# Layer norms by token block, folded scale and shift, an unrolled layer loop, and the next layer's modulation under the feed-forward

## The reference

```python
for l in range(DEPTH):                                  # DEPTH = 2
    mod = c_act @ w_ada[l] + b_ada[l]                   # 6 * 1024 numbers
    sh1, sc1, gt1, sh2, sc2, gt2 = [m[:, None, :] for m in jnp.split(mod, 6, axis=-1)]
    h = x * (1.0 + sc1) + sh1
    y = _token_mixer(h, ...)                            # three attention branches, gates, w_out
    x = _layernorm(ALPHA * x + gt1 * y, ln_g[l, 0], ln_b[l, 0])
    h = x * (1.0 + sc2) + sh2
    y = _conv_ffn(h, w_up[l], w_conv[l], b_conv[l], w_down[l])
    x = _layernorm(ALPHA * x + gt2 * y, ln_g[l, 1], ln_b[l, 1])
```

## Time and profile before

| | |
|---|---|
| median of 3 runs | 3110.49 us (3108.21 to 3115.19) |
| profiled execution, device time | 3112.35 us |
| its span, first to last instruction | 3110.7 us |
| mean granted TensorE clock | 0.908 |
| TensorE, weight loads, VectorE, ScalarE busy | 87%, 74%, 71%, 47% |
| mean transfer rate over the span | 216 GB/s |

### The profile page before, as it was taken

One profiled execution on the slowest core, in us unless ns is written; L12 is line 12 of the kernel. 1 busy time (PEld: TensorE's weight loads), 2 busy tenths in 40 slices (PEclk: granted clock), 3 DMA queues, 4 the chain that ended last, 5 costly groups with the idle time before them and its releaser, 6 DMA issues.

```text
span 3110.7 us, 39930 instructions
## 1 busy us (share of the span) xinstructions
PE 2692.7 (87%) x13946; PEld 2286.7 (74%) x13946; DVE 2210.7 (71%) x2764; ACT 1471.9 (47%) x1677; POOL 19.6 (1%) x38
## 2 busy tenths in 40 slices
PE   5888877976888769968888996759999999999997
PEld 4766757965666659958787975658888888888885
DVE  6666656868666657855576545459889898898986
ACT  3243434423244334425333423337777777777774
POOL 0000000000000000000000000000000000000000
PEclk7899988987899889978898987669999999999998
DMA  8633335558533335533204563129898898898985
GB/s 316 253 139 122 137 121 179 185 184 310 215 127 122 132 125 190 198 128 109 82 15 146 178 228 119 55 97 363 343 364 341 340 365 340 337 366 339 370 337 210
DMA packets 104027, 670.75 MB, mean 216 GB/s; under 512 B 11920, under 2 KB 12048, under 8 KB 26432
## 3 DMA queue, kind: packets, MB, share of 16 engines
q1 hardware_dynamic: 98032, 629.95, 54.8%
q0 software_dynamic: 5840, 38.80, 3.3%
HBM read 664.51 MB, written 4.19 MB: 215 GB/s over the span
## 4 chain that ended last, share of the span: by engine, by line
PE 52%; DVE 16%; PEld 16%; issue 8%; ACT 5%; DMA 2%; DVEq 0%; PEldq 0%; SPq 0%; ACTq 0%
PE bank L762 15%; PE bank L763 15%; PE bank L764 15%; PEld bank L764 5%; PEld bank L762 5%; PEld bank L763 5%; DVE W_low L1780 4%; PE bank L1064 3%; DVE work L1827 2%; ACT W_high L1413 1%; DMA W<-in_w_expert 1%; ACT scores L1459 1%; PEld bank L1295 1%; DVE scores L1967 1%; PE bank L819 1%
## 5 line engine op out<-in xcount | busy, mean ns | idle before, releaser
L1780 DVE TENSOR_TENSOR W_low<-W,W_high 128x1024 fp32r<-128x1024 f32 (+2 forms) x448 | 519.9, 1203 | 373.3 <-ACT W_high L1413 366.3
L1413 ACT ACTIVATE W_high<-W 128x1024 fp32r<-128x1024 f32 (+2 forms) x448 | 442.9, 1037 | 669.1 <-PE bank L764 272.0
L763 PE MATMUL bank<-W_low,arena_parts 128*128 128x512 f32 x1224 | 481.9, 394 | 0.0
L762 PE MATMUL bank<-W_high,arena_parts 128*128 128x512 f32 x904 | 365.0, 404 | 26.9 <-DVE work L2282 20.2
L762 PE MATMUL bank<-W_high,hT_high 128*128 128x512 f32 (+4 forms) x784 | 322.6, 412 | 47.0 <-DVE arena L1767 19.0
L764 PE MATMUL bank<-W_high,arena_parts 128*128 128x512 f32 x904 | 357.2, 395 | 0.0
L762 PE MATMUL bank<-hT_high,W_high 128*128 128x256 f32 x1184 | 344.3, 291 | 13.7 <-DVE hT_low L1800 11.8
L763 PE MATMUL bank<-hT_low,W_high 128*128 128x256 f32 x1184 | 340.2, 287 | 0.0
L764 PE MATMUL bank<-hT_high,W_low 128*128 128x256 f32 x1184 | 339.9, 287 | 0.0
L763 PE MATMUL bank<-W_low,hT_high 128*128 128x512 f32 (+4 forms) x784 | 311.5, 397 | 0.0
L764 PE MATMUL bank<-W_high,hT_low 128*128 128x512 f32 (+4 forms) x784 | 310.6, 396 | 0.0
(11 more groups left out here) (338 smaller groups left out, 4491.1 us busy)
## 6 DMA issues: line engine op xcount, KB each, us to landing
W<-in_w_expert SPq DMA_DIRECT2D x192, 1024.0 KB, 4.8
W<-in_w_layer SPq DMA_DIRECT2D x178, 1024.0 KB, 5.0
arena<-in_w_expert SPq DMA_DIRECT2D x144, 1024.0 KB, 4.8
W<-in_w_middle SPq DMA_DIRECT2D x58, 1024.0 KB, 5.0
arena<-in_w_layer POOLq DMA_DIRECT2D x32, 1024.0 KB, 7.6
R<-in_rows_layer SPq DMA_DIRECT2D x70, 256.0 KB, 5.8
R<-in_rows_middle SPq DMA_DIRECT2D x18, 256.0 KB, 6.1
spread<-arena POOLq DMA_DIRECT2D x1, 3072.0 KB, 11.9
```

Of the source, the lines that this page charges most:

```text
L762: mm(bank, lhs[0], rhs[0], start=start, stop=False)
L763: mm(bank, lhs[0], rhs[1], start=False, stop=False)
L1413: do(high_slot(a.at, w)[:, cols], raw(a.at, w)[:, cols], ACT.Copy).then_inc(main_highs.filled[main_highs.slot(a.at, w)], 1)
L1780: tt(lows(v.at, w)[:, cols], raw(v.at, w)[:, cols], high_slot(v.at, w)[:, cols].bitcast(F32), ALU.subtract).then_inc(*low_ready.event(v.at))
```

## The change

- The layer loop is written out twice (`LAYERS`), on all engines.
- `layernorm` is replaced by `stat(t)` inside `residual` (aggregate one block as soon as its two banks are in), `roots` (one root per block on ScalarE), `norm` (reciprocal, subtract and scale in quarters; each signals `h_ready`, and TensorE transposes that quarter), and `scale_x`, which applies g and b to x later: under the first two `up` tiles, or behind the next transposed tiles.
- The transposed rows are not those of the finished x: g, b and the modulation are folded into one scale and one shift per column (`fold`, tiny products on [128, 8]; g and b in column form come with `adac`, `nextc`, `lnc`), and `shifted` applies them on VectorE while it takes the tiles from PSUM. ScalarE's `high_shifted` makes the high part, VectorE the low one. In the middle, where there is no modulation, g and b are applied so.
- `up` starts when the first half of the columns is split (`group_split` of after + NT) and waits for the second half in the middle of its first group.
- `down` ends bank by bank: for the last four k tiles each bank gets all four before the next.
- Some weights have their high part in free places of the arena (`EARLY`), and the first two weights of the next part are split before the last residual (`high_next`, `low_next`).
- Modulation chunks 10 and 11 and, in layer 0, the next layer's chunks 2, 3, 0 and 1 are made in single steps between the tiles of `up` and `down` (`ada_steps`, `next_column`, `next_in`); their weights come over POOL's queue.
- SP issues a row two weight loads later than before, and at the start constants and x behind the first two weights. The lambda row is worked on after chunk A 0. The output is written in two halves.

```diff
+        EARLY = {("layer0", ("up", 0, 0)): 10256, ("layer0", ("up", 1, 0)): 12304,
+                 ("layer1", ("up", 0, 0)): 10256, ("layer1", ("up", 1, 0)): 12304,
+                 ("layer1", ("A", 0, 0)): 2048, ("layer1", ("A", 0, 1)): 16400,
+                 ("middle", ("ba", 0, 0)): 2048, ("middle", ("qkv", QKV[0], 0)): 16400,
+                 ("middle", ("up", 0, 0)): 6144, ("middle", ("up", 1, 0)): 8192,
+                 ("middle", ("wq", 0, 0)): None}
...
+                for c in range(tiles // 2 - 2):
+                    for k in (2 * c, 2 * c + 1):
+                        ready(k)
+                        for j in range(4):
+                            last = row(k, j)
                             hand_back()
...
+                for j in range(4):
+                    for k in range(tiles - 4, tiles):
+                        if j == 0:
+                            ready(k)
+                        last = row(k, j)
...
+            def shifted(name, scale, shift):
+                for q in range(2):
+                    for t in range(NT):
+                        dve.wait_ge(*psum.full(v.at, (name, t, q)))
+                        bank = banks[psum.slot(v.at, (name, t, q))]
+                        for i in range(4):
+                            f = 4 * q + i
+                            o = ts(hT[:, f, t * P:(t + 1) * P], bank[:, i * P:(i + 1) * P], scale[:, f:f + 1],
+                                   shift[:, f:f + 1], ALU.mult, ALU.add)
...
+                    for t in range(NT):
+                        state["group"] += 1
+                        dve.wait_ge(*group_high.nth(v.at, state["group"]))
+                        f, cols = slice(4 * q, 4 * q + 4), slice(t * P, (t + 1) * P)
+                        tt(hT_low[:, f, cols], hT[:, f, cols], hT_high[:, f, cols].bitcast(F32), ALU.subtract
+                           ).then_inc(*group_split.event(v.at))
...
+            def norm(signal=None):
...
+                for n in range(2):
+                    for t in range(NT):
+                        if n == 0:
+                            invert(t)
+                        half = x[:, t, n * 512:(n + 1) * 512]
+                        i = ts(half, half, meanvar[:, t, 0:1], inv[:, t:t + 1], ALU.subtract, ALU.mult)
...
+                norm(h_ready)
+                shifted("h2T", modc[:, 64:72], modc[:, 72:80])
+                steps_ = ada_steps(l)
+
+                def between_up(j):
+                    if j < 2:
+                        scale_x(v.at, "ln1", j)
+                        return
+                    for _ in range(2 if j > 9 and j % 2 else 1):
+                        next(steps_, None)
...
+                hidden_conv(FF1 // P, hid1, taps_kept, between_up)
+                for c in range(FF1 // 256 - 2):
+                    low(1)
+                    for _ in range(3):
+                        next(steps_, None)
...
+                low_next(LAYERS[l + 1] if l + 1 < DEPTH else "middle", 2)
                 residual(DOWN, 2, ALPHA)
-                layernorm("ln2")
+                norm(h_ready)
...
+                else:
+                    shifted("hT", modc[:, 80:88], modc[:, 88:96])
+                    for n in range(2):
+                        scale_x(Pass(LAYERS[l - 1]), "ln2", n)
```

More of the change, by code:

```diff
@@ L49 @@
 NEG = -1.0e30
-PASSES = (("start", 1), ("layer", DEPTH), ("middle", 1), ("expert", NE - 1), ("last", 1), ("over", None), ("end", 1))
+LAYERS = tuple(f"layer{l}" for l in range(DEPTH))
+PASSES = (("start", 1),) + tuple((p, 1) for p in LAYERS) + (
+    ("middle", 1), ("expert", NE - 1), ("last", 1), ("over", None), ("end", 1))
 OVER = 2 * S // (P + 1)
@@ L565, in high_vacant @@
                 return weights.vacated(at, SPLIT[at.part][i - 2])
-            slot = weights.slot(Pass("layer"), SPLIT["layer"][i - 2])
-            return weights.freed[slot], at.value(weights.users(slot), 1)
+            before = PASSES[[p for p, _ in PASSES].index(at.part) - 1][0]
+            return weights.vacated(Pass(before), SPLIT[before][i - 2]) if SPLIT[before] else (weights.freed[i], 1)
         def raw(at, w):
@@ L2611, in _ @@
             residual(DOWN, None, ALPHA)
-            layernorm("ln2")
-            low_tiles("wxT", 2, hTs)
+            norm(h_ready)
+            shifted("wxT", modc[:, 16:24], modc[:, 24:32])
+            for n in range(2):
+                scale_x(v.at, "ln2", n)
             for c in range(2):
```

734 lines of the change are left out of this document (431 added, 303 removed).

## The result

The changed kernel takes 3089.72 us in the median of four executions (3082.64 to 3091.38), beside 3109.68 us for the kernel before on the same chip: a ratio of 0.9928, 95% interval 0.9908 to 0.9948. It is faster, by 20 us and not by 61, and the range of 3028 to 3078 does not hold the time.

A forecast was written before the change was run, and what follows sets the result against it. TensorE is busy 87%, so only its pauses, mainly at seven normalisations, could be won: gains 88.6 less losses 27.1, net 61.5 us, giving 3049 us. Forecast range 3036 to 3062 (0.50); 3028 to 3078 eight times in 10.

The forecast's parts named there:

- A 0 1 can only be loaded when down 8 is freed (about E-11): Layer 0 to 1, E being the last product's end: second weight ready about E-2.6, pause 54.2 to 12.9, saving 41.3 us.
- Rival 4: Pauses do not shorten as drawn, something else arrives last: 10 to 20 us lost over seven places, 3059 to 3069; chance 0.16.
- the prediction's terms for them: Layers' feed-forwards: modulation steps overfill VectorE, stalling TensorE 5.1 and 3.8 us in layer 0, 2.2 in layer 1.
- That split is over before E: ln1 of a layer: next stage's last weight split before the last product ends, transposes from E+3.5, second half ready E+14.0.
- the 12.2 saved of the prediction: ln1 of a layer: net saving per layer after the second pause and 1.1 us for the clock; 24.4 us for both.
- (d): A/B chunk stage: moved lambda work costs 1.5 us per layer, ln2 passes 1.3 more in layer 1; 4.3 us.
- (e): Start: constants and x issued later, VectorE's first step waits until 23.6, shift follows both splits; costs 5.5 us.
- (b): Layer 0's down stage: modulation slot refills land 1.0 us late five times; costs 2 us (bounds 0 and 20).
- (c): End of down: bank-by-bank finish wants down 10 before its halves are ready; 1.4 us three times, 4.2 us.
- 1 (the cover holds): Feed-forwards: VectorE's steps overlap more and splits keep their lead, so 17.3 us of costs vanish, 3032; chance 0.15.
- 2 (transfers): Layer 0's down stage: SP and POOL transfers compete, landing grows, 15 to 40 us more, 3064 to 3089; chance 0.15.
- 3: Feed-forwards: double buffering of modulation slots fails, work queues behind waiting steps, 120 us, 3169, slower than before; chance 0.02.

The follow-up runs named there:

- experiment 1: Changed kernel with the four weight slots handed out on across the parts instead of beginning again at slot 0: 3066.78 us, ratio 0.9858.
- Experiment 2: Changed kernel with the banks of ada 10 and 11 freed earlier and the next modulation's first column made later: 3077.00 us, ratio 0.9891.
- Experiment 5: Changed kernel without seven of eight VectorE steps of each modulation chunk; sums become other numbers: 3206.12 us in all, layer feed-forwards 201.9 and 196.6 us.
- Experiment 9: Experiment 4 plus one step a tile in layer 1, second weights' low halves behind the norm, constants' row awaited later at the start: 3043.62 us, ratio 0.9783.
- experiment 6: Changed kernel with the products of down in the old order, all four banks ending with the last tile: 3083.07 us, ratio 0.9907.
- experiment 8: Experiment 4 plus modulation steps spread otherwise and second weights' low halves behind the norm, with down in the old order: 3062.90 us, ratio 0.9843.
- experiment 4: Changed kernel with slots handed out on across parts, banks of ada 10 and 11 freed earlier and the first column later: 3053.50 us, ratio 0.9814.

## Why the prediction was wrong

**The boundaries (23.7 us of the miss).** The failing step is the sentence "A 0 1 can only be loaded when down 8 is freed (about E-11)". I took the ring to run on; it begins again in each part, so A 0 0 waits for down 9 and A 0 1 for down 10, the residual starts at E+11.4 and not ahead of E, and with the count running on the kernel is 22.9 us faster (experiment 1). The rest of the chain was right in kind: with the slots running on the pauses are 15.2 and 15.5 us (predicted 12.9 and 18.2), and the first is longer at least in part because the second weight took 9.3 us to arrive and not 5 (experiment 1). The sign that the prediction named as the gravest, a boundary that keeps more than 20 us, is what came. Rival 4 named this mechanism, "a weight of A 0 landing after E", and put 10 to 20 us on it; it was 24. I gave it 0.16 although the slot of a load can be worked out from the counts in the code, and the profile of the kernel before had no row on which the question hung.

**The feed-forwards of the layers with their ln1 (20.4 us).** Four steps, of which two were not in the prediction at all, the bank and the columns:
- The bank of ada 10 (not in the prediction). I priced VectorE's steps as lateness of the weights' low halves and never asked who else waits for the moved evictions. Experiment 2 puts 9.1 + 2.7 us on the bank, the column and the low clock behind them. The sign named for this stage, pauses of 1 to 3 us in front of up tiles after the tenth, came as one of 5.47 us at a bank. With bank and column out of the way the steps cost some 4.4 and 2.4 us (206.3 and 199.0 against 201.9 and 196.6 without steps); the prediction's terms for them were 8.9 and 2.2, so that layer 0's was too large.
- The columns (not in the prediction). I took them out of the boundary and put them nowhere. Their 32 products keep TensorE 4.5 us in layer 0's feed-forward:

```profile
L939 PE MATMUL bank<-consts,arena 128*128 128x1 f32 x32 | 4.5, 261 | 2.7 <-DVEq L1961 2.7
```

- ln1. "That split is over before E" was wrong: in layer 0, with E = 463.99, it is in the way as before, and two residual blocks follow it.

```profile
463.04 2.35 DVE L1861 TENSOR_TENSOR W_low<-W,arena_parts 128x1024 fp32r<-128x1024 f32 x2
...
468.02 0.68 DVE L2072 TENSOR_TENSOR work<-bank,arena 128x512 f32<-128x512 f32 x1
...
471.30 3.49 PE L851 MATMUL bank<-consts,x 128*128 128x128 f32 x16 [7.31 <-DVE x L2038]
...
476.93 0.38 PE L794 MATMUL bank<-hT_high,arena_parts 128*128 128x256 f32 x1 [2.14 <-DVE hT_low L1889]
480.96 0.55 PE L794 MATMUL bank<-hT_high,arena_parts 128*128 128x256 f32 x1 [1.88 <-DVE hT_low L1889]
```

Transposes start at E+7.3 (predicted E+3.5), the second half is ready at E+17.0 (predicted E+14.0): 3.0 us in each layer. The pause before the first product, 12.9, looks like the 12.2 saved of the prediction and is not: that number already held the second pause. From the transposes to the second half it took 9.7 us, where 10.5 was predicted; the shifting tensor_scalar took 0.33 us (eight in 2.64), forecast 0.37.
- The clock behind every restart. I had charged 1.1 us for it at the start of the stage, and nothing for the pauses inside it. Stretches of layer 0's feed-forward at 0.50, behind the first products, the bank and the column, with one at 1.00 from before the first product:

```profile
474.47:477.88 3.41, 1.27 (x11) 1.03 (x10) 3.31 (x10) 1.03 (x2) 0.00 (x0) 1.00 0.03 14
477.88:484.71 6.83, 4.95 (x24) 4.69 (x23) 2.84 (x7) 1.26 (x2) 1.05 (x2) 0.50 0.33 112
600.76:607.59 6.83, 6.14 (x29) 6.17 (x30) 5.11 (x9) 2.42 (x3) 0.52 (x1) 0.50 0.80 306
624.66:631.48 6.82, 6.82 (x20) 5.66 (x21) 6.35 (x11) 0.42 (x1) 0.39 (x1) 0.50 0.61 226
```

TensorE worked 17.9 us at the low level, where it had worked 3.7 before. As a product that comes every 0.12 us comes every 0.21 there, I estimate 8 to 9 us lost against 1.6 to 1.9. Of these 6 to 7 more, only some 0.6 falls at the start of the stage, which the 1.1 covered; the others fall behind the bank and the column and are part of what experiment 2 is about. With pauses of 12.0 us behind the first product (before: none) and the columns' 4.5, this makes some 23 of the 24.7 us by which the stage grew.

In these rows the clock does not wait for products: between E and 476.93 TensorE ran nothing but the sixteen transposes, from 471.30 to 474.79, and the granted clock was 1.00 from 474.47 to 477.88, and fell to 0.50 while the first products ran. The Trainium skill (TensorE: Matmul & The Clock Gate, Part 4: PE-mode transpose) has it that transposes do not count as work for the clock. This place does not agree: in the changed kernel and in every experiment the clock rose 3.1 to 3.3 us behind the first transpose, before any product. The kernel before agrees: there the same sixteen came in two groups with 1.0 us between them, and the clock stayed at 0.50 from 475.25 to the first products. What makes the difference was not settled. The row that the prediction cites against that rule, the window from 1892.40 on at 0.95, says less than it made of it, since the products from 1890.99 to 1892.40 still ran at 0.50.

Experiment 5 bounds what is not the steps: without the steps, ln1 and feed-forward are 10.1 and 4.7 us above my sum for them (214.7 against 204.6, 209.4 against 204.7), of which 3.0 each are ln1 and 4.5 the columns. The rest, 2.6 and 1.7, is near the short pauses that are left in these stages (0.97 and 1.28 us; 0.79 and 0.53).

**What was better than forecast, and what only looks so.** (d), the lambda and scale passes, shows as 1.2 us in the table, where 4.3 were forecast. But TensorE's pauses in these stages grew by 4.3 us in the two layers together, as forecast; the clock gave back the rest, which is luck (the same stages took 825.6 to 830.8 us in the other profiles, 0.3 us less to 4.9 more than before). (e), the start, cost 2.8 instead of 5.5. VectorE waited for the row of constants, as predicted, but the step that was forecast for 23.6 came at 21.63:

```profile
21.40 0.20 DVE L2160 COPY modc<-R 128x64 f32<-128x64 f32 x1 [9.11 <-DMA R<-in_cols_layer]
```

Experiment 9, which moved this wait and two low halves, took 3.3 us back. (b) did not come: VectorE never waited for a transfer into its modulation slots in the changed kernel's 476 to 720 us. (c), 1.4 us for down 10, showed as a pause of 1.05 us in layer 1 and in the middle. But the gain that it was paid for came nowhere, as experiment 6 shows; experiment 8 shows that it comes once nothing stands ahead of the residual. The middle's first part, 4.1, is the clock, not the change, since its pauses are the same.

**The rivals.** 1 (the cover holds) fell with pauses of 5.5, 2.7 and 3.3 us inside the up stages, where there had been none; 2 (transfers) had no wait of VectorE for a transfer to stand on; 3 did not occur. With the two faults mended (experiment 4) the kernel takes 3053.5 us, inside the forecast's own range of 3036 to 3062. That is in part luck: the columns and the later ln1 are still in it, and the steps, the start and the clock were kinder than forecast.

## What to carry to other kernels

When work is moved ahead of a boundary, work out by hand which slot of each ring its transfer gets and whose last use frees that slot; where counting begins again in each part, the first loads of a part can fall on the slots freed last. A product, a load or an eviction put into another stage must be placed where its input is ready on the slower engine, and it holds a bank for that long: the losses found here came from such places, and placing them again, with the second weights behind the norm, won 56 us over the changed kernel. A gain behind an in-order queue is worth nothing until everything ahead of it in that queue is early, so an edit that measures zero may pay after the next one (the finish by banks: nothing, if not a small loss, then 11 us).

## What the runs showed of the hardware that I had not expected

A pause of 3.3 us of TensorE at the same place brought the granted clock down in one execution and not in the other, 86 products in 12 us against 63. Pauses of 5.5 and 2.7 us within the up stage both led to windows at 0.72. The middle's first part, with the same 34.1 us of pauses in every profile, spread over 6 us. So a stage with pauses can differ between executions by more than many edits are worth, and the pauses alone, span less busy time of TensorE, tell an edit's effect better than the stage's time.

At ln1 of layer 0 transposes alone brought the granted clock up: 0.50 until 3.2 us behind the first of sixteen, then 1.00, with no product run in between. In the kernel before they did not.
